# Prompt attention of a decoder step: sixteen units over three probability buffers, issued in runs, one row in four scaled by GpSimd

## The reference

```python
def dense_attend(q, q_pos, k, v, k_pos, rel_bias, window):
    ...
    s = jnp.einsum('bqgrd,bkgd->bgrqk', q, k).astype(jnp.float32) * SCALE + bias.astype(jnp.float32)
    s = jnp.where(valid, s, NEG_INF)
    p = jax.nn.softmax(s, axis=-1) * jnp.any(valid, axis=-1, keepdims=True)
    o = jnp.einsum('bgrqk,bkgd->bqgrd', p.astype(v.dtype), v)
    return o, p
...
    o_att = (g[:, :, 0] * o_c + g[:, :, 1] * o_s + g[:, :, 2] * o_w).reshape(B, T, D_ATT)
```

## Time and profile before

| | us |
|---|---|
| median of 3 runs | 1743.6 |
| the 3 runs | 1743.35, 1743.6, 1747.5 |
| the profiled execution, its own time | 1745.86 |
| its span, from the first to the last instruction | 1744.1 |
| PE busy in the span | 1674.6 (96%) |
| DVE, ACT, POOL busy | 1312.2, 679.7, 373.1 |

### The profile page before, as it was taken

How to read it: one execution, slowest core, us unless ns; L and a number is a source line. 1 busy time by engine, 2 the same in 40 slices (tenths; PEclk the granted TensorE clock), 3 DMA queues, 4 the chain that set the end, 5 groups by cost and what they waited for, 6 DMA issues and landing times.

```text
span 1744.1 us, 30945 instructions
## 1 busy us (share of the span) xinstructions
PE 1674.6 (96%) x11785; PEld 1568.7 (90%) x11785; DVE 1312.2 (75%) x2686; ACT 679.7 (39%) x1061; POOL 373.1 (21%) x369
## 2 busy tenths in 40 slices
PE   7999998779899999999999999999999999999997
PEld 5699965459799999999999999999999999999997
DVE  0435546764777799998999999949878787878786
ACT  1335523762422234443344444433333333333332
POOL 3211000000000001111444455422223222222220
PEclk9999986999999999999999999999999999999998
DMA  9787576000633157776899999999999999999991
GB/s 341 262 271 277 206 233 242 1 1 1 242 99 107 39 159 272 240 232 205 306 386 388 383 383 385 384 365 383 401 369 345 343 346 340 352 337 349 341 320 62
DMA packets 178038, 466.45 MB, mean 267 GB/s; under 512 B 20398, under 2 KB 92334, under 8 KB 176250
## 3 DMA queue, kind: packets, MB, share of 16 engines
q1 hardware_dynamic: 130298, 289.53, 46.8%
q0 software_dynamic: 44880, 172.82, 27.0%
q10 hardware_dynamic: 2736, 2.49, 0.5%
HBM read 408.21 MB, written 63.37 MB: 270 GB/s over the span
## 4 chain that ended last, share of the span: by engine, by line
PE 86%; DVE 7%; DMA 3%; ACT 2%; issue 1%; ACTq 1%; POOL 0%; DVEq 0%
PE ps L1136 31%; PE ps L1022 26%; PE ps L748 10%; PE ps L975 3%; PE ps L1115 2%; PE ps L653 2%; ACT arena L1179 2%; PE ps L626 1%; PE ps L946 1%; DVE arena L1730 1%; DVE ul L1882 1%; PE ps L875 1%; PE ps L938 1%; DMA gr<-gw 1%; PE ps L1031 1%
## 5 line engine op out<-in xcount | busy, mean ns | idle before, releaser
L1882 DVE TENSOR_TENSOR ul<-raw,uh 128x1024 fp32r<-128x1024 f32 x256 | 311.8, 1223 | 109.5 <-ACT uh L1179 108.0
L1022 PE MATMUL ps<-hh,uh 128*128 128x392 f32 x1024 | 357.7, 349 | 1.8 <-DVE ul L1882 1.7
L1022 PE MATMUL ps<-hl,uh 128*128 128x392 f32 x1024 | 350.1, 342 | 0.0
L1022 PE MATMUL ps<-hh,ul 128*128 128x392 f32 x1024 | 348.1, 340 | 0.0
L1136 PE MATMUL ps<-ah,ul 128*128 128x392 f32 x1000 | 342.0, 342 | 0.0
L1136 PE MATMUL ps<-al,uh 128*128 128x392 f32 x1000 | 341.1, 341 | 0.0
L1136 PE MATMUL ps<-ah,uh 128*128 128x392 f32 x1000 | 339.8, 340 | 1.1 <-DVE al L2105 1.1
L1179 ACT ACTIVATE uh<-raw 128x1024 fp32r<-128x1024 f32 x256 | 269.9, 1056 | 101.4 <-PE ps L1136 88.1
L558 POOL DMA_INDIRECT xT<-in_u,gidx x128 | 176.7, 1380 | 546.2 <-DVE zg L1930 332.3
L558 POOL DMA_INDIRECT xT<-in_v,gidx x128 | 136.8, 1069 | 378.3 <-DVE vacc L2119 360.9
L1179 ACT ACTIVATE zbuf<-ps 128x392 f32<-128x392 f32 x128 | 63.7, 498 | 360.8 <-PE ps L1022 360.6
(11 more groups left out here) (380 smaller groups left out, 2343.0 us busy)
## 6 DMA issues: line engine op xcount, KB each, us to landing
raw<-in_uT SPq DMA_DIRECT2D x128, 512.0 KB, 5.8
raw<-in_v SPq DMA_DIRECT2D x128, 512.0 KB, 6.3
gw<-stage POOLq DMA_DIRECT2D x28, 896.0 KB, 11.0
gr<-gw SPq DMA_DIRECT2D x32, 784.0 KB, 8.3
zs<-zbuf SPq DMA_DIRECT2D x124, 196.0 KB, 5.7
zin<-zs SPq DMA_DIRECT2D x124, 196.0 KB, 5.9
arena<-in_ada_w SPq DMA_DIRECT2D x32, 512.0 KB, 4.4
arena<-in_w_in SPq DMA_DIRECT2D x18, 512.0 KB, 6.5
```

The costliest lines, as they stand in the source:

```text
L1022: last = mm(ps[:, bank, 0:DN], w[x][:, k * P:(k + 1) * P], m[:, k, G0:TOK], start=(k == 0 and x == 0 and m is hh), stop=(k == KD - 1 and x ...
L1882: tt(ul[:, i % 4, :], raw[:, i % 4, :], uh[:, i % 4, :].bitcast(F32), SUB).then_inc(S["lo_done"], 1)
```

## The change

- **Buffers.** `pbuf` gets three sets of rows (`u % 3`), `ptb` two sets of four slots (`u % 2`).
- **Sign.** The reduction multiplies by -1 and takes the minimum, so `pst(u, 0)` holds the negated maximum at once; the operation on L1735 and the semaphore `u_max` go. The exponential gets `scale=-1.0`, and each waits for its own row's reduction (`u_ttr`) instead of the unit's maxima.
- **ACT's order.** Two exponentials of unit `u + 1`, three weightings of unit `u`, two exponentials of unit `u + 1`.
- **POOL.** The fourth row of each unit is multiplied by its factor on GpSimd (`u_last`), 16 instructions in all.
- **PE's order.** Up to two transpose groups of unit `u`, all values of unit `u - 1`, the other transpose groups of unit `u`, the scores of unit `u + 3`. The scores of units 1 and 2 come before the first transposes.
- **DVE's order.** Two reductions of unit `u + 2`, the factor of unit `u + 1`, two copies of unit `u`, two reductions of unit `u + 2`, two copies of unit `u`. The copy out of a finished query block comes one unit later than before; the last one stays behind the two subtractions.

The diff, cut to its core:

```diff
-        pbuf = at(34064, 2 * GRP, SEQ)
-        ptb = at(13520, 4, GRP * P)
+        pbuf = at(34064, 3 * GRP, SEQ)
+        ptb = at(13520, 8, GRP * P)
...
+            for u in range(16):
+                pool.wait_ge(S["u_rs"], u + 1)
+                row = pbuf[:, (u % 3) * GRP + 3, 0:(units[u][0] + 1) * P]
+                pool.tensor_scalar(row, row, pst(u, 3)[:, 3:4], None, MUL).then_inc(S["u_last"], 1)
...
+            def turn(u, kb):
+                if kb == 0:
+                    pe.wait_ge(S["u_p"], 3 * (u + 1))
+                    pe.wait_ge(S["u_last"], u + 1)
+                n = first_turn[u] + kb
+                if n >= 2:
+                    pe.wait_ge(S["u_tdone"], n - 1)
...
+            for u in (1, 2):
+                for j in range(GRP):
+                    score(u, j)
             pe.wait_ge(S["pc_tdone"], 4)
...
+            for u in range(17):
+                blocks = units[u][0] + 1 if u < 16 else 0
+                for kb in range(min(2, blocks)):
+                    turn(u, kb)
+                if u >= 1:
+                    for kb in range(units[u - 1][0] + 1):
+                        add_values(u - 1, kb)
+                for kb in range(2, blocks):
+                    turn(u, kb)
+                if u + 3 < 16:
+                    for j in range(GRP):
+                        score(u + 3, j)
...
+                act.wait_ge(S["u_ttr"], GRP * u + r + 1)
+                fn(row, row, ACT.Exp, scale=-1.0, bias=pst(u, 0)[:, r:r + 1], accum_out=pst(u, 2)[:, r:r + 1]).then_inc(S["u_exp"], 1)
...
+            for r in range(GRP):
+                exponential(0, r)
+            for u in range(16):
+                if u < 15:
+                    exponential(u + 1, 0)
+                    exponential(u + 1, 1)
+                for r in range(3):
+                    weigh(u, r)
+                if u < 15:
+                    exponential(u + 1, 2)
+                    exponential(u + 1, 3)
...
-                                             1.0, -3e38, ADD, MAX, pst(u, 0)[:, j:j + 1]).then_inc(S["u_ttr"], 1)
-                dve.wait_ge(S["u_ttr"], GRP * (u + 1))
-                ts(pst(u, 1), pst(u, 0), -1.0, None, MUL).then_inc(S["u_max"], 1)
...
+                                         -1.0, 3e38, ADD, MIN, pst(u, 0)[:, j:j + 1]).then_inc(S["u_ttr"], 1)
...
+            for j in range(GRP):
+                ttr(1, j)
+            scale(0)
+            for u in range(16):
+                for j in range(0, GRP, 2):
+                    if u + 2 < 16:
+                        ttr(u + 2, j)
+                        ttr(u + 2, j + 1)
+                    if j == 0 and u + 1 < 16:
+                        scale(u + 1)
+                    evac(u, j)
+                    evac(u, j + 1)
+                if u % 4 == 0 and u > 0:
+                    out_moved(u // 4 - 1)
```

More of the change, by code:

```diff
@@ L882, in _, with score @@
                     [(11 + kb, P, lambda b, kb=kb: vwin[:, b * 4 + kb, :]) for kb in range(4)])
[L884 removed]
+            def score(u, j):
                 i, br, w = units[u]
[L886 to L891 removed]
+                r, g = heads(w)[j]
+                if u >= 1:
+                    pe.wait_ge(S["u_ttr"], GRP * (u - 1) + j + 1)
+                mm(ps[:, j, 0:(i + 1) * P], zT[half(g), QC + r, i * P:(i + 1) * P], zT[half(g), (KS, KW)[br], 0:(i + 1) * P],
+                   start=True, stop=True).then_inc(S["u_s"], 1)
             pe.wait_ge(S["att_dve"], 5)
@@ L918, in _ @@
             last.then_inc(S["os_ready"], 1)
-            scores(0)
+            for j in range(GRP):
+                score(0, j)
             pe.wait_ge(S["os_done"], 2)
@@ L925, in _ @@
                 turn_cached(i)
-            tcount = [0]
-            def apply(u):
-                i, br, w = units[u]
-                pe.wait_ge(S["u_p"], GRP * (u + 1))
-                for kb in range(i + 1):
-                    n = tcount[0]
-                    if n >= 2:
-                        pe.wait_ge(S["u_tdone"], n - 1)
-                    for r in range(GRP):
-                        last = pe.transpose(ps[:, 4 + n % 2, r * P:(r + 1) * P],
-                                            pbuf[:, (u % 2) * GRP + r, kb * P:(kb + 1) * P], ident[:, :])
-                    last.then_inc(S["u_t"], 1)
-                    tcount[0] += 1
-                for kb in range(i + 1):
-                    pe.wait_ge(S["u_tdone"], tcount[0] - i + kb)
-                    pt = ptb[:, kb, :].rearrange("p (r g q) -> p r g q", g=2, q=P)
-                    for g in range(2):
-                        last = mm(ps[half(g), 6 + i % 2, 2 * w * P:2 * (w + 1) * P], vn[:, br * 4 + kb, half(g)], pt[:, :, g, :],
-                                  start=False, stop=(br == 1 and kb == i))
-                last.then_inc(S["u_pv"], 1)
@@ L950, in _ @@
-            pe.wait_ge(S["pc_tdone"], 4)
-            for i in range(4):
-                for q in range(4):
-                    u = 4 * i + q
-                    if u < 15:
-                        scores(u + 1)
-                    if q == 0 and i >= 2:
-                        pe.wait_ge(S["o_done"], i - 1)
-                    if q % 2 == 0:
-                        cols = slice(q * P, (q + 2) * P)
-                        for g in range(2):
-                            mm(ps[half(g), 6 + i % 2, cols], vc[0:NCMP_P, 8, half(g)],
-                               ptcb[0:NCMP_P, i, g * 512:(g + 1) * 512][:, cols], start=True, stop=False)
-                    apply(u)
+            first_turn = [sum(i + 1 for i, _, _ in units[:u]) for u in range(16)]
@@ new lines, in turn @@
+            def turn(u, kb):
[6 more added lines that the diff above has]
+                for r in range(GRP):
+                    last = pe.transpose(ps[:, 4 + n % 2, r * P:(r + 1) * P],
+                                        pbuf[:, (u % 3) * GRP + r, kb * P:(kb + 1) * P], ident[:, :])
+                last.then_inc(S["u_t"], 1)
@@ new lines, in cached, with add_values @@
+            def cached(i, w):
+                cols = slice(2 * w * P, 2 * (w + 1) * P)
+                for g in range(2):
+                    mm(ps[half(g), 6 + i % 2, cols], vc[0:NCMP_P, 8, half(g)],
+                       ptcb[0:NCMP_P, i, g * 512:(g + 1) * 512][:, cols], start=True, stop=False)
+            def add_values(u, kb):
+                i, br, w = units[u]
+                if kb == 0 and u % 4 == 0 and i >= 2:
+                    pe.wait_ge(S["o_done"], i - 1)
+                if kb == 0 and br == 0:
+                    cached(i, w)
+                pe.wait_ge(S["u_tdone"], first_turn[u] + kb + 1)
+                pt = ptb[:, (u % 2) * 4 + kb, :].rearrange("p (r g q) -> p r g q", g=2, q=P)
+                for g in range(2):
+                    last = mm(ps[half(g), 6 + i % 2, 2 * w * P:2 * (w + 1) * P], vn[:, br * 4 + kb, half(g)], pt[:, :, g, :],
+                              start=False, stop=(br == 1 and kb == i))
+                if kb == i:
+                    last.then_inc(S["u_pv"], 1)
```

80 lines of the change are left out of this document (34 added, 46 removed).

## The result

| | before | after |
|---|---|---|
| median, us | 1745.55 (4 runs) | 1725.37 (4 runs) |
| lowest to highest | 1743.35 to 1748.04 | 1719.73 to 1727.2 |
| the profiled execution, its own time | 1745.86 | 1723.57 |
| its span | 1744.1 | 1721.9 |
| the stage, first reduction to first matmul of the projection | 101.80 | 79.13 |

The account below looks back on a forecast made before the run. PE's own work was to bound the stage: opening 4.7, work 64.7, waits 4.1, way to projection 3.0, low clock 4.5, together 81.0 us instead of 101.8. That gave 1722.8 us, range 1717 to 1733 (forecast's own case 1717 to 1731).

Parts of the forecast that it names:

- The bound and the sum: First reduction to projection: PE's work becomes the bound, terms sum to 81.0 us instead of 101.8, 20.8 less.
- PE's waits: In the stage: 4.1 us remain, before second score pairs of units 3, 5, 7, 9 and transposes of 14, 15.
- The low clock: PE in the stage: the same 18 us at half rate as before, costing the new order 4.5 us.
- rival 2: PE's clock stays low: until 36 us into the stage 1731, until 63 us today's time; chance 0.09, to 1738.
- The opening and the tail: Stage's ends: 4.7 us to first transposes; 3.0 from last values, or 4.9 from last copy, to projection.
- GpSimd was mis-sized: POOL's fourth-row multiplication: 0.7 us at 512 columns, between 0.6 and 1.13, hidden beside ACT's three weightings.
- The threshold of 1.85 us: POOL's row at 512 columns costs nothing while under 1.85 us, the time of ACT's three weightings.
- rival 5: GpSimd rows over 1.85 us make PE wait; over 7 us gives back the whole gain; slower, chance 0.04.
- Rival 1: Handovers between engines bind: 0.6 us more in each of 16 units, stage 90.6 us, time 1732; chance 0.08.
- Rival 3: DVE's reduction with -1 and minimum is slower: at double length stage about 99 us, time 1741; chance 0.03.
- Rival 4: First GpSimd row starts late: a 3 us delay adds 1.7 to the end, giving 1725; chance 0.04.
- The code load: GpSimd's first call: about 6 us in a freshly loaded kernel, adding 4.1 us to the end, 1727.

Follow-up runs that it names:

- e12: The changed kernel itself, unaltered, run again in later rounds: median 1720.62 us, 0.9841 of the kernel before, stage 79.00 us.
- e10: The changed kernel plus 18 idle identity transposes into an unread PSUM bank in PE's opening gaps: 1720.99 us, ratio to before 0.9841, stage 76.43.
- e4: The changed kernel with PE's values of a unit behind all its own transposes again: 1726.96 us, ratio to before 0.9883, stage 89.08.
- e8: The kernel before with only the sign trick and each exponential waiting for its own row: 1740.69 us, ratio to before 0.9971, stage 100.80.
- e2: The changed kernel with GpSimd's row made twice as long by an extra multiplication by one: 1718.09 us in one run, stage 79.29.
- e3: The changed kernel with GpSimd's row made four times as long by three extra multiplications: 1745.89 us in one run, stage 98.10.
- e1: The changed kernel with each unit's fourth row weighted by ACT again, no GpSimd: 1720.19 us, ratio to before 0.9851, stage 79.79.
- e6: The changed kernel with the sign operation and the wait for all four maxima put back: 1757.82 us, ratio to before 1.0068, stage 113.27.
- e11: e10 plus the projection's two subtractions moved ahead of the last two copies: 1716.18 us, ratio to before 0.9825, stage 74.90.

## Why the prediction was right, step by step

The forecast was 1722.8 us and the median is 1725.37; 20.8 us less were predicted and 20.2 came. That the totals agree so closely is partly luck: the stage gave 22.7 us, not 20.8, and in e12's rounds the same kernel was 29.1 us under the one before. The mechanism is what held. The steps:

- **The bound and the sum.** The stage was forecast at 81.0 us, 4.5 of them for the low clock, so at 76.5 without it. e10, at 1.00 throughout, took 76.43. No large errors cancel in that: the opening took 4.65 us (4.7 forecast), PE's work and waits to the end of the last values 68.5 (64.7 + 4.1), and the way to the projection 3.25 (3.0). PE's durations, read from the earlier trace rows, were right in the new order.
- **PE's waits.** I forecast 1.4, 0.6, 1.1 and 0.3 us before the second score pairs of units 3, 5, 7 and 9 and 0.4 each before the transposes of units 14 and 15 (4.2 in all, not 4.1). In e10's timeline these runs of eight last 1.4, 0.6, 1.0 and 0.4 us longer than undisturbed ones, and the last two waits are 0.44 each. Those two had the right size for the wrong reason: I wrote that they would be for ACT, and the profile names DVE's copies out of the transpose banks. Here are units 3, 5 and 6; the second is 1.73 us long where the third has 1.13:

```profile
287.20 0.49 PE L894 MATMUL ps<-arena 64*128 64x128 f32 x4
288.58 0.70 PE L894 MATMUL ps<-arena 64*128 64x128 f32 x4 [0.89 <-DVE cst L1766]
...
293.19 1.73 PE L894 MATMUL ps<-arena 64*128 64x256 f32 x8
...
296.60 1.13 PE L894 MATMUL ps<-arena 64*128 64x256 f32 x8
```

- **The low clock was the term that was off.** I let the new order keep 18 us at half rate, 4.5 us of loss. It had about 10 us of it, worth 2.6 (79.00 against 76.43). The difference, 1.9 us, is that by which the stage came in under its forecast. The 4.2 us that the old order is said to lose stays an estimate: no run kept the kernel before at 1.00. The clock rises about 13.4 us into the stage, so "1.00 from its second quarter" holds until the tail. Nor did rival 2 come; the runs show it as a cost that depends on the order, larger in e4 and e8 and absent in e10.
- **The opening and the tail** kept their lengths: 4.65 us to the first transposes (4.7 forecast), and from the start of the last copy to the projection again 4.9.
- **GpSimd was mis-sized, and it cost nothing.** I took 0.7 us for a row of 512 columns between bounds of 0.6 and 1.13. It takes 1.56 us, above both. The step that failed is the scaling from iotas and a masked copy: neither has this operation's cost per column. The Trainium skill (GPSIMD Engine Reference, section "4.1 Engine selection") has one-input work at about line rate, and the estimate from the same page's 1.03 cycles per element (its section 3.1), 0.44 us, is 3.5 times too low; the measurement decides. The threshold of 1.85 us failed as well: 3.2 us a row were still hidden (e2). I had compared POOL with ACT's weightings, but PE comes for the unit later than both. At 334.14 + 1.56 = 335.70 us a row was done, and PE began to transpose at 338.65. The far end of rival 5 held: its forecast was that over 7 us a row give back the whole gain, and 6.5 us do so almost (e3, one run).
- **Rival 1**, slower handovers, did not come: PE waits 1.4 us before transposes in the whole stage. **Rival 3** fell with the row of 686 ns. **Rival 4** fell with POOL's first row, which takes 0.61 us, as long as the later ones, and follows DVE's factor at once. The code load of the Trainium skill (GPSIMD Engine Reference, section "2.1 Instruction dispatch") is not seen here:

```profile
287.87 0.61 POOL L553 TENSOR_SCALAR arena<-arena,cst 128x128 f32<-128x128 f32 x1 [54.68 <-DVE cst L1770]
```

- **Who waits for whom.** I expected idle time on ACT and DVE released by PE. DVE's is (6.0 us of it before the copies). ACT's 19.8 us are released by the reductions, one link further on.
- **What was not in the forecast:** PE's clock over the projection's first matmuls. 24 of them took 5.47 us in the changed kernel and 4.57 in the one before; where the clock is at 1.00 they take 3.03. The first had a wait of 3.28 us ahead of it instead of 2.20, but the length of that wait doesn't settle it: behind 3.25 us the 24 took 3.04 in e1 and e2, 4.31 in e10, 4.58 in e3 and 5.47 in e6. What does stays open.
- **Two readings that were off** without touching the sum: the 2.30 us that the prediction puts before the projection is the wait of the transposes at 376.49, the projection's was 2.20; and a copy has 512 columns in every block (686 ns), so in block 0 only the activations are mostly fixed cost (389 ns at 128 columns, 710 at 512).

## What to carry to other kernels

Walk each engine's written order with durations from the trace of before, and let every instruction wait for its engine and its semaphores: that gave this stage, in which PE, ACT and DVE were all reordered, within 0.1 us at the full clock. The handover for single rows alone shortened the stage by 1 us, the new order without it left PE's waits as long as before and lengthened the stage by 11 (nearly all of it PE's busy time at a lower clock), and together they shortened it by 22.7; so price such parts jointly, and look for the ring that the old wait would close in the new order. What a helper engine must keep to is the time at which its consumer comes for the piece, and not the duration of the work beside it; in the two runs here a row shorter than the consumer's time per unit was hidden, and a longer one set the pace. And compare idle time beside totals, since a variant that idles more may also lose clock (e6: 19 us of one and 15 of the other).

## What the runs showed of the hardware

- A multiply by a per-partition factor on GpSimd, float32 in SBUF, takes 603, 923, 1243 and 1562 ns for 128, 256, 384 and 512 columns on 128 partitions. ACT's weighting of 512 columns takes 0.62 us (three from 350.01 to 351.86 us in the changed kernel). GpSimd's work did not slow DVE's: copies of 512 columns took 688 ns and reductions 686 with POOL busy for 69.4 us of e3's stage, and 686 and 686 with POOL idle in e1.
- In the changed kernel TensorE's clock fell to 0.50 in the opening, around idle times of 0.98 and 1.19 us, and stayed there for about 10 us, 7 of them with PE busy without a gap. PE's timeline there:

```profile
284.59 1.12 PE L894 MATMUL ps<-arena 64*128 64x128 f32 x8 [0.98 <-DVE cst L1759]
286.90 1.43 PE L894 MATMUL ps<-arena 64*128 64x128 f32 x8 [1.19 <-DVE cst L1759]
288.89 1.09 PE L942 MATMUL ps<-ident,arena 128*128 128x128 f32 x4 [0.56 <-ACT arena L1197]
```

Eighteen idle transposes in these gaps kept it at 1.00 through the stage in both kernels that had them (e10, e11). How long it stays low differed from 10 us (after) to 24 us (e8), and no run settles what sets that length.
